# Leaving out the products of constants that fill TensorE's waits in a three-layer transformer kernel

## The reference, cut to what matters

```python
# layer 0: conformer convolution, then the experts
h = x @ w_pw1 + b_pw1; a, gate = split(h, 2); h = a * sigmoid(gate)
h = depthwise_conv(h, w_dw, width=31) + b_dw
x = layer_norm(ALPHA * x + silu(layer_norm(h)) @ w_pw2 + b_pw2)
x = layer_norm(ALPHA * x + grouped_moe(x))     # 16 experts, 4 groups, top 2 by a router
# layer 1: differential attention, 8 heads, with k, v = x @ w_kv, then the same experts' step
x = layer_norm(ALPHA * x + diff_attention(x))
x = layer_norm(ALPHA * x + grouped_moe(x))
# second block
proj = rmsnorm(x) @ w_in        # attention over the top 64 keys, an hgrn2 scan, a short convolution, gates
x = x + mixed(proj) @ w_out
x = x + square(relu(rmsnorm(x) @ w_mlp_up)) @ w_mlp_down
```

## The kernel before

| call | what comes next | products |
|---|---|---|
| L1555 | `pw1`, the first linear step | 3 |
| L1628 | `pw2`, after `bias_lines(0)` | 4 |
| `tile_T`, t = 0, layer 0 and 1 | transposes for the router | 2 each |
| L1675, layer 0 and 1 | ranking of the tokens | 2 each |
| `norm_T("ln1", ..., 8)` L1835 | transposes, then `k` of the attention | 8 |
| `norm_T("rm0", before=12)` L2006 | transposes, then `ikw`, `akv`, `aq` | 12 |
| `norm_T("rm1", before=4)` L2193 | transposes, then the MLP | 4 |

## Time and profile before

### The profile page before, as it was taken

One profiled execution on the slowest core, in us unless ns is written; L12 is line 12 of the kernel. 1 busy time (PEld: TensorE's weight loads), 2 busy tenths in 40 slices (PEclk: granted clock), 3 DMA queues, 4 the chain that ended last, 5 costly groups with the idle time before them and its releaser, 6 DMA issues.

```text
span 1282.5 us, 16097 instructions
## 1 busy us (share of the span) xinstructions
PE 1196.0 (93%) x6536; PEld 855.8 (67%) x6536; DVE 641.8 (50%) x949; ACT 477.8 (37%) x741; POOL 205.3 (16%) x190
## 2 busy tenths in 40 slices
PE   7998999999988998999999989989999789999998
PEld 7986754344435986744444336879887676888996
DVE  3897631212115678711222125694389884545544
ACT  3496421011103566211111013465566433434442
POOL 6000000000002000000000000185788451000000
PEclk9999989999999999799999998999999899999999
DMA  9900879999998540889999994433344331364450
GB/s 333 326 1 1 346 294 430 426 429 427 428 413 283 190 145 26 339 368 428 427 429 426 427 376 152 144 131 132 132 149 178 126 138 66 131 229 165 175 219 33
DMA packets 68162, 321.23 MB, mean 250 GB/s; under 512 B 4071, under 2 KB 12660, under 8 KB 55418
## 3 DMA queue, kind: packets, MB, share of 16 engines
q1 hardware_dynamic: 64944, 308.57, 60.8%
q0 software_dynamic: 2592, 11.42, 2.5%
q10 hardware_dynamic: 554, 0.23, 0.1%
HBM read 317.02 MB, written 3.18 MB: 250 GB/s over the span
## 4 chain that ended last, share of the span: by engine, by line
PE 69%; DVE 17%; ACT 5%; DMA 5%; issue 3%; POOL 1%; DVEq 0%; SPq 0%; ACTq 0%
PE bank L1527 31%; PE bank L1710 23%; PE bank L1592 4%; PE bank L1701 3%; DMA arena<-in_moe_w_up_dram 2%; DMA ring<-in_w_kv_dram 2%; PE bank L1759 2%; DVE w_lo L666 2%; POOL w_lo L666 1%; PE bank L1495 1%; ACT w_hi L953 1%; DVE arena L2292 1%; DVE rows L2846 1%; DVE arena L2865 1%; PE bank L1599 1%
## 5 line engine op out<-in xcount | busy, mean ns | idle before, releaser
L666 POOL TENSOR_TENSOR w_lo<-ring,w_hi 128x512 fp32r<-128x512 f32 (+1 forms) x124 | 176.6, 1455 | 668.8 <-ACT w_hi L953 668.8
L953 ACT ACTIVATE w_hi<-ring 128x2048 fp32r<-128x2048 f32 (+1 forms) x102 | 192.0, 1883 | 218.6 <-PE bank L1527 217.1
L666 DVE TENSOR_TENSOR w_lo<-ring,w_hi 128x2048 fp32r<-128x2048 f32 x71 | 160.8, 2266 | 150.6 <-ACT w_hi L953 150.1
L1527 PE MATMUL bank<-x_hi,w_hi 128*128 128x256 f32 x672 | 111.7, 289 | 3.8 <-DVE x_lo L2247 2.2
L1527 PE MATMUL bank<-x_hi,w_lo 128*128 128x256 f32 x672 | 108.7, 284 | 0.8 <-POOL w_lo L666 0.7
L1527 PE MATMUL bank<-x_lo,w_hi 128*128 128x256 f32 x672 | 108.3, 284 | 0.0
L1527 PE MATMUL bank<-w_hi,x_hi 128*128 128x512 f32 (+1 forms) x336 | 95.9, 400 | 9.4 <-DVE x_lo L2627 3.6
L1710 PE MATMUL bank<-arena 128*64 128x512 f32 x352 | 98.6, 594 | 1.9 <-ACT arena L953 1.8
L1527 PE MATMUL bank<-w_lo,x_hi 128*128 128x512 f32 (+1 forms) x336 | 94.9, 398 | 4.8 <-POOL w_lo L666 4.7
L1527 PEld LDWEIGHTS bank<-x_hi,w_hi 128*128 128x128 f32 x672 | 92.9, 192 | 6.4 <-issue 5.9
L953 ACT ACTIVATE arena<-bank 128x512 f32<-128x512 f32 (+3 forms) x85 | 40.0, 486 | 146.2 <-PE bank L1743 103.9
(11 more groups left out here) (333 smaller groups left out, 1779.0 us busy)
## 6 DMA issues: line engine op xcount, KB each, us to landing
ring<-in_w_in_dram SPq DMA_DIRECT2D x15, 2048.0 KB, 8.0
ring<-in_moe_w_gate_dram SPq DMA_DIRECT2D x12, 2048.0 KB, 19.8
arena<-in_moe_w_down_dram SPq DMA_DIRECT2D x12, 2048.0 KB, 21.6
arena<-in_moe_w_gate_dram SPq DMA_DIRECT2D x12, 2048.0 KB, 17.3
ring<-in_moe_w_down_dram SPq DMA_DIRECT2D x12, 2048.0 KB, 18.3
ring<-in_moe_w_up_dram SPq DMA_DIRECT2D x12, 2048.0 KB, 17.5
arena<-in_moe_w_up_dram SPq DMA_DIRECT2D x12, 2048.0 KB, 21.3
wslots<-in_moe_w_up_dram SPq DMA_DIRECT2D x8, 2048.0 KB, 22.4
```

The source lines that it names most:

```text
L666: last = ops.tensor_tensor(part(w_lo, label, hb)[:, x].bitcast(F32R), ring_half(label, hb)[:, x], part(w_hi, label, hb)[:, x], ALU.subtract)
L953: return s.activation(dst, src, ACT.Copy)
L1527: last = mm(bank(use_)[:, at:at + cols], still, moving, start=start and opens and (hb, n, k) == (0, 0, 0), stop=stop and closes and (hb, n ...
```

## The change

The loop that issues the products is taken out of `warm`. The nine calls stay, and each still waits for its bank.

```diff
             def warm(label, times, moving=masks, cols=HALF):
 
                 claim(pe, label)
-                for _ in range(times):
-                    mm(bank(label)[:, 0:cols], ident[:], moving[:, 0:cols], start=True, stop=True)
```

## The result

| | before | after | |
|---|---|---|---|
| runs with the first result (7 and 7) | median 1286.13, 1284.3 to 1289.6 | median 1293.36, 1290.9 to 1295.9 | ratio 1.0042, 95% interval 1.0028 to 1.0056 |
| timed again (35 and 12) | median 1287.40, 1284.4 to 1291.2 | median 1292.23, 1290.6 to 1298.7 | 1.0043, 1.0027 to 1.0059 |
| profiled execution | 1284.22, span 1282.5, clock 0.976 | 1291.29, span 1289.6, clock 0.963 | +7.07 us |

Leaving the products out costs 0.42%, some 5.5 us. (The ratios are those on record; the quotients of the medians alone, 1.0056 and 1.0037, lie on either side of them.) The prediction said slower, and 1293.4 lies between its 1289 and 1305; but its sum was +12.1 us, more than twice the cost, and "slower by over 0.5%" had 0.84 of the chance where the measured ratio is just under that.

What follows compares the result with a forecast made beforehand. The chain was taken as mostly TensorE's own products, with the clock nearly always at its upper level. Terms summed to +12.1 us: 1296.3 against the profiled execution, 1298.2 against the median; 1297 taken, range 1289 to 1305.

Steps and rivals of the forecast that it cites:

- the tempting 15 us: Across the kernel: products of constants hold some 15 us of the chain, but mostly fill waits, so removal would not win it.
- rm0: Call with 12 products: no direct gain; ten slow transposes +1.1, twelve slow 68-column groups +2.7, earlier clock return -0.5; sum +3.3 us.
- pw2: Call with 4 products ahead of the linear step: no direct gain, 5 us of idle, then low clock; +2.1 us.
- ln1: Call with 8 products: no direct gain; slow transposes +0.6, then `k`'s 256-column stream at low clock +2.0; sum +2.6 us.
- rm1: Call with 4 products: no direct gain; slow transposes +1.0, then the MLP's 256-column stream at low clock +2.0; sum +3.0 us.
- pw1: Call with 3 products at the start: direct gain 0.4 us against a likely low clock behind; taken +0.6 us.
- Experts: Calls with 2 + 2 products per layer: layer 0 -0.5 + 1.2 = +0.7 us, layer 1 -0.2 us.
- the stream's charge: 4.5 us of low clock per dense stream behind over 4 us idle: 2.1 us for 512 columns, 2.0 for 256.
- (a): Rival: the clock falls at some places only; if pw1, pw2 and rm1 stay fast, 1291 us; chance 0.13.
- (b): Rival: the clock stays low longer, each of four streams taking 3.5 us more; 1303 to 1304 us; chance 0.10.
- (c): Rival: not slower, as real work sets the clock; only direct gains of -1.1 stand; 1283 to 1285 us; chance 0.05.
- (d): Rival: faster, as the chain's 15 us of products are truly on the path; 1270 us; chance 0.02.

## Why the prediction was wrong in size

- **What bounds the kernel, and the tempting 15 us:** right. Nothing came back from the products on the chain, except at `tile_T`: 0.5 us forecast in layer 0, 0.6 in the traces that leave out that call alone.
- **The price of a low clock:** right. 128x512 groups took 1.7 us and 68-column groups 0.86; for 256 columns, estimated at a loss of 0.44 a microsecond, the low groups start 0.85 apart against 0.48, which is the same 0.44. For `rm0`'s ten transposes the prediction put +1.1, where its own 0.21 and 0.12 us each make 0.9; the traces have 1.1.
- **"I charge 4.5 us of low clock for each dense stream that begins behind an idle stretch of over 4 us":** this step failed. It holds for `pw2`, where the stream follows the idle directly (+1.8 measured, 2.1 forecast). At `ln1` and `rm1` sixteen transposes stand between, the same sixteen whose slowness I had priced (+0.6 and +1.0, measured +0.6 and +0.7), and they bring the clock back before the first product (seven traces of seven at each place). `ln1`: 2.6 forecast, +0.6 measured from behind the drop at 392. `rm1`: 3.0 forecast, +1.4, since in three traces of seven the clock fell a second time. I had the row that shows it, and even argued from it at `pw1` against the page's rule, but did not carry it to the other two places. The Trainium skill's rule (TensorE: Matmul & The Clock Gate, Part 4: PE-mode transpose), that transposes do not engage the full clock, is contradicted again: four of them leave the stream low for 5.7 us, sixteen bring the clock up before a product has run at `ln1`, `rm0` and `rm1`. At `pw1` they do so in ten traces of 18 only, so the row that I followed there was one of two outcomes.
- **rm0:** transposes +1.1 as forecast; the 68-column groups cost 0 or 1.6 instead of 2.2, since they too began at the upper level.
- **pw1:** 0.6 forecast, 0.9 found in the difference; against the profiled execution, in which the start was at its best, 1.85.
- **Experts:** +0.7 and -0.2 forecast against the profiled execution, +0.8 and -0.3 in the traces. Layer 0's small products became like layer 1's, as forecast: 2.26 us to the first gather (from 169.01 to 171.27) in the changed kernel's trace.
- **The sum was set against one execution.** It had `pw1`, the experts, `ln1` and `rm1` at their best, so everything the change could lose showed as a loss, while an average execution with the constants has already lost 0.9, 0.6, 0.6 and 0.2 there. I noted that it was 1.9 us below the median and did not ask which places that came from. With 0.5 at `rm0` and -0.3 in layer 1's experts this makes 2.5 of the 6.5 us by which the sum was too high. The other 4.0 lie between the forecast terms and the traces' means against that execution: `ln1`, `rm0` and `rm1` cost 5.0 less than forecast, through the stream's charge, and `pw1` 1.2 more.
- **Rivals:** (a), the clock falling at some places only, at 1291, was nearest, with the wrong mechanism: it fell nearly everywhere but came back sooner. (b) is out: each of its four streams cost less than the sum had for it. (c) is out, and (d) too.

What stays open: whether `rm0`'s 1.1 us reach the end. Two timings gave -1.4 and +1.2 us, and single places are at the edge of what these timings can resolve, as the runs of one kernel spread by 7 us. Several drops inside the experts and the scan fall at other places from execution to execution, apart from the change; whether leaving out one group of constants shifts those systematically was not tried. Open too is why sixteen transposes brought the clock back in time at every other place, but at `pw1` in ten traces of 18 only, and what makes it fall a second time at `rm1`.

## What to carry to other kernels

Price work that fills a wait by what runs next: a dense stream directly behind the idle time gains from it, a stream behind a block of some 3 us of transposes gained little at three places here, since that block ran slowly but brought the clock back. At the start of the kernel it did so only in some traces, so look at more than one. Compare places with the same places in several traces and not with one execution, which may be the lucky one; the local distances show costs of 1 to 2 us, and add up to about the timed effect, where no single timing could resolve them. A product of constants is not free either: where nothing is late it sits on the path, and at the low level it sits there for longer.

## What the runs showed of the hardware

Sixteen 128x128 transposes took 3.25 to 3.65 us at the low level and 1.94 at the upper (`rm0`, `rm1`). At `ln1`, `rm0` and `rm1` the clock was back 2.8 to 4.1 us after the first of them, at the latest 0.5 us behind the last; at the start of the kernel it was so in ten traces of 18 and took over 8 us in the others. After four, in 0.6 to 1.1 us, it stayed low for another 5.6 to 5.7 us of dense products. A stream that had started at the upper level fell 1 us in, for 3.4 us, in three traces with 1.85 to 1.90 us of idle time ahead of it. The same kernel ran from 1284.1 to 1291.5 us, and traces differ in where 3.4 us long stretches of low clock fall.
